# Three products for four in the key half of a block compression, and one PSUM bank where two took turns

## The reference

```
def compress_rows(rows, pe, w1, w2):          # rows [B, S, G, D]; G = 2, D = 64
    ch = rows.reshape(B, n_chunks, 16, G, D)  # 256 chunks of 16 tokens per sample
    proj = einsum('bnsgd,psdh->pbngh', ch, w1)        # two taps p, hidden h = 256
    bias = einsum('psd,psdh->ph', pe, w1)
    h = proj[0, :, 0:n_blk] + bias[0]
    h = h + proj[1, :, 1:1 + n_blk] + bias[1]         # block n: tap 0 of chunk n, tap 1 of chunk n + 1
    return einsum('bngh,hd->bngd', silu(h), w2)

kc = compress_rows(kv_all[:, :, 0], pe[0], w1[0], w2[0])   # key half
vc = compress_rows(kv_all[:, :, 1], pe[1], w1[1], w2[1])   # value half
```

## Time and profile before

| | |
|---|---|
| runs before | 2232.06 us median of 3 (2231.8 to 2240.67) |
| profiled execution: span from its first to its last instruction | 2233.0 us |
| PE busy / DVE / ACT / POOL over the span | 2092.5 / 1471.5 / 1004.9 / 607.8 us |
| granted TensorE clock, mean | 0.969 |
| steps of the samples | about 380 to 964 us of the span |

### The profile page before, as it was taken

How to read it: one execution, slowest core, us unless ns; L and a number is a source line. 1 busy time by engine, 2 the same in 40 slices (tenths; PEclk the granted TensorE clock), 3 DMA queues, 4 the chain that set the end, 5 groups by cost and what they waited for, 6 DMA issues and landing times. The chain is left out here.

```text
span 2233.0 us, 41102 instructions
## 1 busy us (share of the span) xinstructions
PE 2092.5 (94%) x16006; PEld 1877.4 (84%) x16006; DVE 1471.5 (66%) x3233; ACT 1004.9 (45%) x2112; POOL 607.8 (27%) x932
## 2 busy tenths in 40 slices
PE   6999999999999999996789898997999999999997
PEld 5999997777777777774678787777999999999997
DVE  4222225777776776786578687558688788765667
ACT  4114223655554664654367486325333333334334
POOL 0001003444443443431069596120111111110000
PEclk9999999999999999986879999998999999999999
DMA  4116565554654654658510011331332332365342
GB/s 128 57 57 186 191 224 168 194 196 163 201 171 133 212 167 149 177 137 276 191 52 8 8 48 48 108 109 41 101 114 75 101 116 77 97 239 193 118 165 97
DMA packets 217338, 295.53 MB, mean 132 GB/s; under 512 B 23474, under 2 KB 160914, under 8 KB 207762
## 3 DMA queue, kind: packets, MB, share of 16 engines
q1 hardware_dynamic: 199736, 191.64, 27.7%
q0 software_dynamic: 17408, 101.26, 13.0%
HBM read 217.12 MB, written 82.63 MB: 134 GB/s over the span
## 5 line engine op out<-in xcount | busy, mean ns | idle before, releaser
L3241 DVE TENSOR_TENSOR a_XTL<-cpt,a_XTH 64x256 fp32r<-64x256 f32 (+1 forms) x576 | 230.5, 400 | 87.9 <-ACT a_XTH L3126 79.5
L3126 ACT CAST a_XTH<-cpt 64x256 fp32r<-64x256 f32 (+1 forms) x576 | 201.4, 350 | 97.5 <-PE cpt L3350 85.3
L3365 PE MATMUL cph<-a_XTH,w1H 128*128 128x512 f32 x512 | 216.0, 422 | 0.0
L3365 PE MATMUL cph<-a_XTL,w1H 128*128 128x512 f32 x512 | 204.4, 399 | 0.0
L3365 PE MATMUL cph<-a_XTH,w1L 128*128 128x512 f32 x512 | 204.1, 399 | 0.0
L1558 POOL TENSOR_TENSOR C<-C,a_mt 128x264 f32<-128x264 f32 x66 | 69.0, 1064 | 404.9 <-ACT C L1643 269.9
L2077 PE MATMUL f<-a_slot,wd_slot 128*128 128x264 f32 x1176 | 148.2, 285 | 2.0 <-DVE a_slot L1887 1.4
L2077 PEld LDWEIGHTS f<-a_slot,wd_slot 128*128 128x128 f32 x1176 | 144.8, 188 | 3.0 <-issue 2.2
L2040 PE MATMUL f<-a_b,ring 128*128 128x264 f32 x1056 | 144.0, 286 | 3.3 <-DVE a_b L1783 2.7
L2040 PEld LDWEIGHTS f<-a_b,ring 128*128 128x128 f32 x1056 | 135.5, 190 | 3.8 <-issue 3.8
L492 PE MATMUL pj<-wH,xL 128*128 128x256 f32 (+2 forms) x464 | 130.9, 282 | 0.0
(11 more groups left out here) (582 smaller groups left out, 5560.7 us busy)
## 6 DMA issues: line engine op xcount, KB each, us to landing
a_slot<-a_T SPq DMA_DIRECT2D x20, 792.0 KB, 4.6
raw<-in_w_in POOLq DMA_DIRECT2D x12, 1024.0 KB
V<-v_s SPq DMA_DIRECT2D x6, 2048.0 KB, 10.3
v_s<-X SPq DMA_DIRECT2D x22, 512.0 KB, 6.0
raw<-in_w_gate SPq DMA_DIRECT2D x22, 512.0 KB, 5.2
raw_odd<-in_w_val SPq DMA_DIRECT2D x22, 512.0 KB, 6.1
a_T<-C SPq DMA_DIRECT2D x20, 528.0 KB, 3.3
a_T<-sums SPq DMA_DIRECT2D x11, 792.0 KB, 4.9
```

Of the source, the lines that this page charges most:

```text
L3126: nc.scalar.copy(turned(XTH, u, s, k, g, a), split(bank(at, k)[:], u, k, g, a)).then_inc(h_ready, 1)
L3241: last = nc.vector.tensor_tensor(turned(XTL, u, s, k, g, a), split(bank(at, k)[:], u, k, g, a), hi.bitcast(F32), ALU.subtract)
L3365: last = nc.tensor.matmul(out[:, :, 0:n], w[:, s, k, q, m * P:(m + 1) * P], x[:, s % 2, k, :, q:q + n], **flags)
```

## The change

**Key half.** Write E and O for the even and odd chunks, A and B for the two taps. A block that begins at an even chunk is A·E + B·O, one that begins at an odd chunk is A·O + B·E of the next pair: four products. Now there are three: A·O, B·E (bank pair `taps`) and (A + B)·(E + O) (bank `joint`); the even blocks are joint - A·O - B·E. A + B is summed once (`wsum`, then its high and low part `ws`), E + O in every step (`low_part`, `high_sum`, `low_sum`). At the end of a sample ACT copies `taps` to `hs` and DVE makes both kinds of blocks there (`join_taps`), before Silu.

**Chunks.** A partition now holds two neighbouring chunks, and a slot of `X` one step (four slots). The gather takes rows of two tokens, twice as many; index tables, overlap table, block maxima and the views in `select` follow that order. A step has 18 + 24 matmuls of 256 columns in place of 24 of 512.

**Banks.** `joint` takes a PSUM bank; the turns are left with one, `pt`. A turn of kind 1 waits until ACT has copied turn 0 (`raw_ready`; the keys are first copied out raw, and their high and low parts are made from the copy); a turn of kind 2 waits until DVE has subtracted turn 1 (`l_ready[1]`); turn 0 of the next step waits for `KTL`. `KTH` and `KTL` have one buffer in place of two. The value projection is cut in two (`project_second(at, 0)` and `(at, 1)`), with the score and turn 2 between.

```
-        pt = [ctx.enter_context(nc.psum_tensor(f"cpt{i}", [P, 512], F32)) for i in range(2)]
+        pt = ctx.enter_context(nc.psum_tensor("cpt", [P, 512], F32))
...
-        ph = [ctx.enter_context(nc.psum_tensor(f"cph{i}", [P, 512], F32)) for i in range(4)]
+        taps = [ctx.enter_context(nc.psum_tensor(f"ctaps{m}", [P, 512], F32)) for m in range(2)]
+        joint = ctx.enter_context(nc.psum_tensor("cjoint", [P, 512], F32))
+        plain = [ctx.enter_context(nc.psum_tensor(f"cplain{m}", [P, 512], F32)) for m in range(2)]
...
         def turn_free(eng, at, kind):
-            n = 3 * at + kind - 2
...
+            if kind == 0 and 1 <= at <= PAIRS:
+                eng.wait_ge(kt_ready, at)
...
+            elif kind == 1 and at < PAIRS:
+                eng.wait_ge(raw_ready, at + 1)
...
+            elif kind == 2:
+                eng.wait_ge(l_ready[1], at + 1)
...
+            def raw_copy(at):
+                act.wait_ge(t_ready[0], at + 1)
+                if at >= 1:
+                    act.wait_ge(l_ready[0], at)
+                for g, a in parts:
+                    last = nc.scalar.copy(part_of(raw[:], at, g, a), split(at, g, a))
+                last.then_inc(raw_ready, 1)
...
+            def high_parts(at, between=None):
+                if at < PAIRS:
+                    raw_copy(at)
+                if at < LAST:
+                    high_part(at, 0)
+                if between:
+                    between()
+                if at < LAST:
+                    high_part(at, 1)
+                if at < PAIRS:
+                    high_sum(at)
+                    keys_high(at)
...
-                for k in range(2):
-                    if at + 1 < LAST:
-                        high_parts(at + 1, k)
-                    if s == NS - 1:
-                        hidden(u, k)
-                keys_high(at + 1)
+                high_parts(at + 1, (lambda: keep_taps(u)) if s == NS - 1 and u < DB else None)
...
+            def low_part(at, k):
+                dve.wait_ge(h_ready[k], at + 1)
+                if k == 1 or at >= PAIRS:
+                    for g, a in parts:
+                        high = part_of(XH[:, at % 2, k, :], at, g, a)
+                        last = nc.vector.tensor_tensor(part_of(XL[:, at % 2, k, :], at, g, a), split(at, g, a), high.bitcast(F32), ALU.subtract)
+                    last.then_inc(l_ready[k], 1)
+                else:
+                    lows(nc.vector.tensor_tensor(XL[:, at % 2, 0, :], raw[:], XH[:, at % 2, 0, :].bitcast(F32), ALU.subtract))
+                    nc.vector.tensor_tensor(raw[:, 0:256], raw[:, 0:256], raw[:, 256:512], ALU.add).then_inc(sum_ready, 1)
...
+            def join_taps(u):
+                for m in range(2):
+                    dve.wait_ge(taps_kept, 2 * u + m + 1)
+                    dve.wait_ge(even_ready, 2 * u + m)
+                    x = hs[:, 0, m]
+                    boths(nc.vector.tensor_tensor(both[:], x[:, :, 0:P], x[:, :, P:2 * P], ALU.add))
+                    boths(nc.vector.tensor_tensor(x[:, :, P:2 * P - 1], x[:, :, 0:P - 1], x[:, :, P + 1:2 * P], ALU.add))
+                    nc.vector.tensor_tensor(x[:, :, 0:P], joint[:, 256 * m:256 * m + 256].rearrange("p (g n) -> p g n", g=NG), both[:], ALU.subtract
+                                            ).then_inc(even_ready, 1)
...
                 turn(at + 1, 0)
-                project(at, 0)
+                project_first(at)
...
-                project(at, 1)
+                project_second(at, 0)
+                score(at)
+                turn(at + 1, 2)
                 if chunk and n >= 1:
                     small_products(n, (2, 3))
-                turn(at + 1, 2)
-                score(at)
+                project_second(at, 1)
```

More of the change, by code:

```diff
@@ L2735, in compress_and_scan @@
         bias = sb("bias", [P, 4])
-        brow = sb("brow", [2, 512])
+        with ExitStack() as views:
+            brow = views.enter_context(nc.sbuf_tensor("a3_brow", [2, 512], F32))
         prow = sb("prow", [P, 2, 256])
+        raw = sb("raw", [P, 512])
+        both = sb("both", [P, NG, P])
         ones = sb("ones", [2, 2])
@@ L2898, in _ @@
             differences(0)
-            gather(2)
             differences(1)
@@ L3016, in _ @@
             sp.dma_start(w2[:], io["cmp_w2"][0].rearrange("k (h p) d -> p k h d", p=P)).then_inc(w_in, 16)
-            for j in range(2):
-                values(j)
+            values(0)
             for at in range(LAST):
@@ L3230, in keep_blocks @@
                     return
[L3231 to L3242 removed]
+                if u >= 1:
+                    dve.wait_ge(c_out, 16 * u)
@@ new lines, in turn, with project_prompt @@
+                last.then_inc(t_ready[kind], 1)
+            three = lambda wH, wL, xH, xL: enumerate(((wH, xH), (wL, xH), (wH, xL)))
+            def project_prompt(at, k):
+                s = at % NS
+                x = lambda X2, q: X2[:, at % 2, k, q:q + P]
+                w = lambda w2, q: w2[:, s, k, q, :]
+                for q in range(2):
+                    for part, (v, y) in three(w(w1H, q), w(w1L, q), x(XH, q), x(XL, q)):
+                        last = nc.tensor.matmul((taps, plain)[k][0][:, 0:256], y, v, start=(s + q + part == 0),
+                                                stop=(s == NS - 1 and q == 1 and part == 2))
+                last.then_inc(mm_ready[k], 1)
@@ L3368, in project @@
-                last.then_inc(mm_ready, 1)
+                    pe.wait_ge(hs_ready[1], u)
+                if u == DB:
+                    if m == 1:
+                        project_prompt(at, 1)
+                    return
+                begins, ends = s == 0, s == NS - 1
+                rows = slice(m * P, m * P + P)
+                out = plain[m][:].rearrange("p (g h n) -> p h g n", g=NG, h=2)
+                for q, h, c in ((0, 0, 0), (0, 1, 256), (1, 0, 256), (1, 1, 1)):
+                    for part, (w, x) in three(w1H[:, s, 1, q, rows], w1L[:, s, 1, q, rows], XH[:, at % 2, 1, c:c + 256], XL[:, at % 2, 1, c:c + 256]):
+                        last = nc.tensor.matmul(out[:, h], w, x, start=(begins and q + h + part == 0), stop=(ends and q + h == 2 and part == 2),
+                                                skip_group_check=True)
@@ L3583, in hybrid_step @@
                     keep["room2"] = raw.enter_context(nc.sbuf_tensor("room2", [P, DB // 2, 2, 4, P], F32))
-                keep["X"] = [later.enter_context(nc.sbuf_tensor(f"X{i}", [P, 2, 4, 512], F32)) for i in range(2)]
+                keep["X"] = later.enter_context(nc.sbuf_tensor("X", [P, 4, 2, 2, 512], F32))
                 later.enter_context(nc.sbuf_tensor("behind_X", [P, 16], F32))
```

415 lines of the change are left out of this document (226 added, 189 removed).

## The result

The changed kernel takes 2385.84 us (median of 4 runs, 2379.61 to 2386.83), the kernel before in the same session 2235.18: a ratio of 1.0672, 95% interval 1.0648 to 1.0695. It is slower by 150 us; 2357 was forecast, with 2300 to 2410. The profiled execution has a span of 2377.8 us against 2233.0, and the 144.8 us between them lie in the compression. The last matmul of the input projections starts at 353.4 us in both, and behind the compression everything runs as before, only later and within about 2 us of its former length.

The account below looks back on a forecast made before the run. PE was taken to bound the kernel before, the one bank's chain after. Chain 105, sample ends less blocks -2, once 3 and clock 19 make 125 us on 2233.0: 2358, or 2357 for the median, range 2300 to 2410.

Parts of the forecast that it names:

- the rival of the clock at its worst: Granted clock falls to the least busy stretch's 0.77, costing 65 us in place of 19; 2403 us, chance 22%.
- PE bounds before, and two banks let the others run behind: In the sample steps PE sets the time, 17.20 us a pair; two banks let ACT and DVE lag a few microseconds.
- The chain of the one bank, 20.47 us per pair: Waits through the single turn bank set each pair of steps: 20.47 us against 17.20, 105 us over 32 pairs.
- even turn 2 to turn 0: Chain piece: turn 0.36, small products 0.26, half a projection 1.42, products to the next turn 0.44; sum 2.48 us.
- Columns on PE, 0.86 us per step: 42 matmuls of 256 columns take 4.96 us against 5.82 for 24 of 512, saving 0.86 us a step.
- the rival on the faster side: PE stays the bound, copies and subtractions always ready in time, 55 us saved over 64 steps; 2181 us, chance 6%.
- `blocks` goes into the stall: In even steps between turn 0 and turn 1, 2.7 of its 3.9 us fall into PE's stall; 19 us in all.
- The end of a sample, 17 us: In a sample's eighth step, tap copies and the join delay turn 2 by some 2.1 us; 17 us for 8 samples.
- Once, 3 us: Summing the weights and making their high and low part before the first steps costs 3 us, bounds 0 and 6.
- the prompt's steps, nothing within 5: Prompt's eight steps, with index tables and views, keep their element counts: no cost, within 5 us either way.
- The clock, 19 us, granted 0.85 to 0.95: PE's stalls in the sample steps lower the granted clock to 0.85 to 0.95, costing 19 us, bounds 0 and 65.
- slot of X came late: Rival: with four one-step slots, gathers come a microsecond late each step, 64 us more; 2421 us, chance 5%.

Follow-up runs that it names:

- e5: Kernel before with one turn bank in place of two, nothing else changed; 2430.09 us, ratio 1.0862.
- e6: Changed kernel, values through a raw tile, scores right behind raw copies, squares last, KTH/KTL before the sums' parts, prompt's values turned through joint; 2233.6 us.
- e3 b: Changed kernel with zero-weight matmuls filling PE's waits ahead of turn 1 in even steps and turn 2 in both; 2400.37 us, ratio 1.0732.
- e1: Changed kernel with two turn banks again, summed-weight products adding into the single products' banks (keys not the reference's); 2288.4 us, ratio 1.0209.
- e7: Changed kernel with two turn banks, and ACT doing raw copies, then scores, squares last, compressed key's high part before the sum's; 2247.44 us.
- e4 with e2: Changed kernel with values copied out raw by ACT alone, and score copies and squares behind the value copies in even steps; 2277.83 us, ratio 1.0181.
- e2: Changed kernel with ACT's score copies and squares moved behind the raw and value copies in even steps; 2369.38 us, ratio 1.0595.

## Why the prediction was right, point by point

The measured 2385.84 us lies in the stated range of 2300 to 2410 and 0.8 us above the forecast's own range of 2325 to 2385. By the number alone the rival of the clock at its worst (2403) is nearer than the forecast (2357); by the mechanism it is out, since it took a granted clock of 0.77 and 0.94 was measured.

*PE bounds before, and two banks let the others run behind.* Shown by e5: the same products with one bank cost 192 us.

*The chain of the one bank, 20.47 us per pair.* It took 21.05. By the pieces, as predicted and as the pair from 706.38 shows: turn 1 to turn 2 3.98 twice, 3.96 and 4.02; odd turn 0 to turn 1 2.48, 2.59; odd turn 2 to `KTL` 1.26, 1.31; `KTL` to the raw copies 4.71, 4.71; raw copies and hand-over 1.58, 1.55. One piece failed: even turn 2 to turn 0, 2.48 against 2.91. No wait stands in it, it is PE's own work:

```profile
725.10 0.33 PE L3579 MATMUL chg<-a_W 128*32 128x32 f32 x16
725.36 0.39 PE L3475 MATMUL cplain<-a_XH,w1H 128*128 128x256 f32 x1
...
727.00 0.27 PE L3579 MATMUL chg<-a_W 128*32 128x32 f32 x8
```

The turn (from 724.52) takes 0.58 us up to the small products where 0.36 had been taken, and half the projection 1.64 where 1.42 had. The reason is the next point.

*Columns on PE, 0.86 us per step.* This term was mis-sized. Without waits an odd step takes 7.49 us in e6 (618.62 to 626.11) and took 8.10: 0.61 less. The pitch of 0.118 us is right, but the first 256-column matmul behind a turn takes longer, and the change makes three such runs of a step's two:

```profile
618.62 0.60 PE L3443 MATMUL cpt<-ident,X 128*128 128x128 f32 x4
618.98 0.36 PE L3473 MATMUL ctaps<-a_XH,w1H 128*128 128x256 f32 x1
619.18 0.28 PE L3473 MATMUL ctaps<-a_XH,w1L 128*128 128x256 f32 x1
619.30 0.28 PE L3473 MATMUL ctaps<-a_XL,w1H 128*128 128x256 f32 x1
```

From the first to the second it is 0.20, then 0.12. The twelve of 512 that were measured as 2.91 had their own such start in them; the 256 pitch came from the middle of a long run and had none. With it the 42 matmuls make 42 x 0.119 + 3 x 0.08 = 5.24 us, against 5.82 a gain of 0.58. In even turn 2 to turn 0 it is likewise the changes from one kind of matmul to the next that cost about 0.1 us each. For the forecast this mattered little, since the saved columns lay in stalls. For the rival on the faster side it did: 64 x 0.58 is 37 us, not 55, and e6, the nearest to it, reached no gain at all.

*`blocks` goes into the stall.* Predicted 2.7 of 3.9 us each; measured 3.3 of 4.2. Before, the five pairs that hold it and no other extra took 21.3 to 21.5 us against 17.18, after 21.5 to 22.4 against 21.05.

*The end of a sample, 17 us.* The pairs that hold it took 22.6 to 25.4 us after, all with some time at the lower level. Seven pairs took 23.9 us over 21.05 in sum. At the 0.41 us of e3 b, their 42.8 us at the lower level are 18 of these, so about 1 us a sample is left for the end itself, less than half of the 2.1 predicted. This is an estimate.

*Once, 3 us; the prompt's steps, nothing within 5.* The score of step 0 comes 4.5 us later (378.6 and 383.1), within the bounds of 0 to 6, that of step 2, one pair on, 8.9 us later (396.2 and 405.1), and from the last score to the end there are 11.0 us more. These last were forecast wrong: element counts stay the same in the prompt, but there too a turn waits for the one bank, between 1102 and 1235 us:

```profile
PE cpt L3413 <- DVE a_XL L3287: 16.2, 7, 4.0
```

Before, turns waited 2.9 us in that part. I had followed the bank through pairs of sample steps only.

*The clock, 19 us, granted 0.85 to 0.95.* It was 0.94. The fit over the 30 pairs gives 0.43 us (standard error 0.19) for each of the 85.3 us at the lower level: about 37 us, 20 to 53; by the 0.41 us of e3 b it is 35. The mechanism is the one that was named, the size about double. By the prediction's own way 0.94 would have cost less still: 6.8 us of a pair divided by 0.94 are 0.4 us more, 14 us in all. But 0.41 of the 0.5 us that a microsecond at that level can take means that most of PE's work there is in the path, not the 6.8 of 20.5 us that were counted. The Trainium skill's rule (Perfetto Trace Analysis, section Matmul Optimizations: the matmul engine scales its power with utilization) agrees in direction: 0.94 with PE busy 81%, where 97% had 0.99. Busy share alone doesn't give the clock, though. It was 0.94 with PE busy 451 of 560 us (changed) and with 506 (e1), 0.97 with 517 (e7) and 0.99 with 501 (e4 with e2). Busy time is itself longer at half the clock; with half of the time at the lower level taken off, these are 417, 470, 502 and 495, still not in the clock's order. What tells them apart, long waits or where they lie, is open.

The sum for the profiled execution, 2358, came out 20 us low. The chain (19 us), the clock (16) and the prompt (11) were under-sized. Against that worked the part of `blocks` that goes into the stall (4), the smaller price of a sample's end (10) and something that the sum did not have: the three pairs with a unit of new tokens took 25.8 us over a regular pair before and 15.7 after, the time at the lower level taken off, so 10 us of their extra work went into stalls too. That errors on both sides nearly cancel is luck; that the chain carries most of the loss is not. No slot of X came late: no wait of PE names a gather.

## What to carry to other kernels

When a change takes a buffer from a pipeline, follow that one buffer through a whole period, with the waits of the engines that empty it, and compare the chain with the bounding engine's own work: how full the engines are says nothing of it. Such a chain is repaired by having the bank emptied by one engine alone (raw copies, from which the parts are made) and by putting these copies ahead of work on the same engine that waits for somebody else; the first edit alone brought 72 us here, the second 16, and all together 152. Price short matmuls from a run of the length that the kernel will have, start included.

## What was not expected of the hardware

- Short waits may cost PE more than themselves: in e1 28.9 us of waits ahead of turns stand beside 78.5 us at the lower clock level, which took about 40 us from PE. In e4 with e2 waits of like size came with 15.3 us at that level only, so it is open when they do.
- The first matmul of 256 columns behind a turn takes 0.20 us to the next, the others 0.12.
- The same subtraction of 512 elements from SBUF on DVE took 0.69 or 0.83 us in nearly every step of the changed kernel, 2.06 to 2.10 in 19 of 64 steps of e2 (741.09, above) and 3.9 to 4.1 in four of e7. In every run, those of 1.6 us and more had POOL at work on `a_W` beside them. That alone does not bring it: in e2 six beside such work took 0.83, and in e6 all but a few stayed at 0.7 to 0.8. What brings it is open.
